# A 1,024-wide RWKV/S5 block with two trunk layers: the last gate projection before the last S5 output, a modulation group behind it

## The chip, the cores and the metric

One core of one Trainium2 chip runs the whole program. The metric is device time in microseconds (us) of one execution; the kernel before was run three times, and its median is 2729.56 us (2729.41 to 2731.32). The core has a matrix engine (TensorE, PE in the profile, with PEld for its weight loads), a vector engine (VectorE, DVE), an activation engine (ScalarE, ACT), a general engine (GpSimd, POOL) and a queue that issues transfers (SyncE, SP). Each engine runs its own instruction list in order, and the lists meet only at semaphores.

## The reference

The input is one sequence of 256 tokens of width 1,024, all in float32. A first block mixes it through two branches, each with a gate, and is followed by a convolutional FFN; then come two trunk layers (gated linear attention, latent attention, convolution, FFN) whose shifts and scales are made from a condition vector. The part that matters here, cut short:

```python
h = rms_norm(x, norm_mix_pre)
proj = h @ w_in                         # rwkv | s5 | gates
gates = sigmoid(proj[..., N_RWKV_COLS + S5_WIDTH:] + b_gate)
g_rwkv, g_s5 = split(gates, 2)          # 1,024 columns each
o_rwkv = rwkv7_branch(...) @ w_branch_rwkv
o_s5 = s5_branch(...) @ w_branch_s5
mixed = (g_rwkv * o_rwkv + g_s5 * o_s5) @ w_out
# s5_branch: a complex scan over time, y = Re(C @ states) + d * u,
#   y = gelu(y);  return y * sigmoid(y @ w_glu + b_glu)
# trunk layers: mod = silu(c) @ w_ada + b_ada   (6,144 columns, twice)
```

## The kernel before

Activations lie with channels on the 128 partitions and the 256 tokens along the free axis. All large weights are cut into tiles of 128x128; eight tiles are a slab of 512 KB, and the slabs lie in memory in the order in which TensorE uses them. SyncE loads slab after slab (L3732) into a ring of six; before it loads slab s it waits until slab s - 6 has been released by TensorE. A projection (`project`, matmul at L904) of 16 tiles takes two slabs and releases the first when it is through with it, the second at its end. A modulation group (`t_ada`, started by `more_ada`, matmul at L1794) multiplies the condition by 512 columns of `w_ada_2`; it takes 32 tiles, four slabs, and releases the four together at its end. All its groups add into one PSUM bank that stays held. No result of a group is read before the first FFN is under way, so a group can stand at many places of the list. The other seven PSUM banks are handed out in turn by `open_job`.

The order of work on TensorE is the order of calls in the list at the end of the program (from L3527 on). In the stretch of interest it is: a loop in which, for every two state tiles of the S5 branch, TensorE computes their inputs (`t_s5bu`, L1550) and one gate projection (`t_gate1`, L904), while VectorE runs the scans (`v_s5scan`, L1563 to L1582). There are eight gate projections of 256 columns, taken in the order GATE_ORDER = (4, 5, 6, 7, 0, 1, 2, 3), seven of them in this loop. After every fourth state tile `t_s5y` (L1593) multiplies the states by C. It waits for the last of the four scans. After the loop stand one modulation group, the last `t_s5y(3)`, and then `t_s5c`, the projection by `w_glu` (L904), which waits for the gelu of ScalarE (L1613), which waits for VectorE's addition of d * u (L1599). Then follow the low-rank products of the RWKV branch (`t_prep`, L1063 on, waiting for ScalarE's tanh at L1029), the Gram matrices (L1193), the triangular inversion (L1232), and the serial stage: four chunks of 64 tokens, each depending on the state of the one before (`t_serial`, L1321 to L1349). Behind it come the eighth gate projection, the group norm of y (`t_y`: L1394 needs ScalarE's copy of the last y at L1379; then two modulation groups; L1400 needs the squares at L1382), two more modulation groups, and `t_merge1`, the branch and output projections (L904), which needs `o_r`, VectorE's last product at L1418.

ScalarE has the same jobs in its own list. `a_gate1` (L1014) applies two sigmoids to a gate projection; the last of them stands in `a_y`, between the copies of y and the squares. Changing between sigmoid, gelu and the logarithm/exponential pair needs a table load on ScalarE. GpSimd loads `rows1`, the low-rank weights, once VectorE has done the addition for the last S5 output (L3709), and the trunk's context once `o_r` is done (L3711). The gates of the eighth projection are read for the first time in the last step of VectorE's merge (`v_merge1`, L1661).

Of the kernel before, what the change touches and what calls it, by code (L numbers as in the profile page):

```python
# [253 lines left out]
def build(nc, t_in, out, known):  # L254
# [3 lines left out]
    with ctx:  # L258
# [15 lines left out]
        def flat(a):  # L274
            return a.rearrange("p a b -> p (a b)")
# [30 lines left out]
        def pc(key, i=0, n=1):  # L306
            c = PCOL[(key, i)] if (key, i) in PCOL else PCOL[key + (i,)]
            return par[:, c:c + n]
# [12 lines left out]
        def at(step):  # L321

            return step_of(step)[1]
# [571 lines left out]
        def project(key, name, l, ms, kt, rhs, n, ready=None):  # L895


            o = open_job(key)
            for i, c in enumerate(ms):
                for k in range(kt):  # L900
                    if ready is not None and i == 0:
                        pe.wait_ge(*step_of(ready(k)))
                    w = tile(name, l, k * P, c)
                    ins = pe.matmul(o[:, i * n:(i + 1) * n], w, rhs(k), start=(k == 0), stop=(k == kt - 1))  # L904
                    slab_done(ins, i == len(ms) - 1 and k == kt - 1)
            ins.then_inc(tensor_jobs, close_job(key))
# [28 lines left out]
        def bank(key):  # L935
            return ps[:, job_of[key], :]
# [19 lines left out]
        def both_tables():  # L956

            act.add_instruction(mybir.InstLoadActFuncSet(name=nc.get_next_instruction_name(), engine=mybir.EngineType.Activation, act_func_set_id=LN_EXP_SET))
# [42 lines left out]
        def t_gate1(j):  # L1001
            c = NRW + RW + 2 * j * P
            project(("g", j), "w_in", 0, [c, c + P], DT, lambda k: h[:, k, :], TX)
# [7 lines left out]
        def a_gate1(j):  # L1011
            act.wait_ge(tensor_jobs, at(("job", ("g", j))))
            for e in range(2):
                act.activation(gates[:, 2 * j + e, :], bank(("g", j))[:, e * TX:(e + 1) * TX], ACT.Sigmoid,  # L1014
                                      bias=pc("b_gate", 2 * j + e)).then_inc(scalar_steps, A.step(("free", ("g", j)) if e else None))
# [149 lines left out]
        GATE_ORDER = (4, 5, 6, 7, 0, 1, 2, 3)  # L1165
# [210 lines left out]
        def a_y():  # L1376
            for c in range(4):
                act.wait_ge(tensor_jobs, at(("job", ("y", c))))
                act.copy(yR[:, :, c * 64:(c + 1) * 64], bank(("y", c))[:, 0:TX].rearrange("p (a b) -> p a b", b=64)).then_inc(scalar_steps, A.step(("free", ("y", c))))  # L1379
            a_gate1(GATE_ORDER[7])  # L1380
            act.wait_ge(vector_steps, at("yc"))
            act.activation(flat(ySq), flat(yC), ACT.Square).then_inc(scalar_steps, A.step("ysq"))  # L1382
            both_tables()
            for j in range(2):
                act.wait_ge(tensor_jobs, at(("job", ("yv", j))))
                act.activation(rstd[:, j, :], bank(("yv", j)), ACT.Ln, bias=eps_col[:, 1:2], scale=1.0 / 64).then_inc(scalar_steps, A.step(("free", ("yv", j))))
            act.wait_ge(scalar_steps, A.n)
            act.activation(flat(rstd), flat(rstd), ACT.Exp, scale=-0.5).then_inc(scalar_steps, A.step("yrstd"))
# [195 lines left out]
        def t_s5y(m):  # L1584

            if m == 0:
                pe.wait_ge(vector_steps, at("cneg"))
            pe.wait_ge(vector_steps, at(("xs", 4 * m + 3)))
            o = open_job(("ys", m))
            for g in range(4):  # L1590
                for q in range(4):
                    c_ = (s5c[:, 0], s5c[:, 1], s5c[:, 1], s5n)[g]
                    ins = pe.matmul(o[32 * q:32 * q + 32, 0:TX], c_[:, 4 * m + q, :], xs[:, q, g, :],  # L1593
                                    start=(g == 0), stop=(g == 3), skip_group_check=True)
            ins.then_inc(tensor_jobs, close_job(("ys", m)))
# [77 lines left out]
        def a_merge1():  # L1673
            for j in range(4):
                a_mixed("wo", "n2", j)
            a_rstd("n2")
# [123 lines left out]
        def more_ada(n=1):  # L1800
            for _ in range(n):
                t_ada(ada_done[0] // ADA, ada_done[0] % ADA)
                ada_done[0] += 1
# [1730 lines left out]
        @block.tensor  # L3534
        def _(tensor):
            nonlocal pe
            pe = tensor
            t_warm()
            t_norm("n1")
            t_proj1("u", (0, 1))  # L3540
            t_proj1("p", (0, 1))
            t_s5bt()
            t_proj1("p", (2, 3))
            t_s5bu(0)
            t_s5bu(1)
            t_proj1("p", (4, 5, 6))
            for p in range(8):
                if p % 2 == 0 and p:
                    t_s5y(p // 2 - 1)
                    more_ada()  # L3550
                if p < 7:
                    t_s5bu(2 * p + 2)
                    t_s5bu(2 * p + 3)
                if p < 7:
                    t_gate1(GATE_ORDER[p])
            more_ada()
            t_s5y(3)
            t_s5c()
            t_prep((more_ada, lambda: t_merge_s5((0, 1)), lambda: t_merge_s5((2, 3))))
            t_tr(("v",))  # L3560
            t_gram()
            t_tr(("At", "Bt", "Kt"))
            more_ada()
            t_chain()
            t_apply()
            t_serial()
            t_gate1(GATE_ORDER[7])
            t_y()
            more_ada(2)
            t_merge1()  # L3570
            more_ada()
            t_norm("n3")
            t_ffn1()
            for l in range(LAYERS):
                n = 512 if l == 0 else TX
                t_gla_in(l, n)
                t_gla(l)
                t_gla_out(l, n)
                t_branch_0(l)
                t_mla(l, n)  # L3580
                t_branch(l, n, 1, "mla_wo_2", lambda k: mO[:, k, 0:n], ahead=GATES_AHEAD)
                t_branch_c(l, n)
                t_wout(l, n)
                t_ln_close(("l1", l), n, more_ada if l == 0 else None)
                t_ffn2(l, n)
                t_ln_close(("l2", l), n)
            while len(stream) % SLAB:
                stream.append(None)

        @block.scalar  # L3590
        def _(scalar):
            nonlocal act
            act = scalar
            act.wait_ge(vector_steps, at("consts"))
            a_norm("n1", xT, ready=lambda k: "loaded_x%d" % (k // 4))
            act.wait_ge(loaded["par"], at("loaded_par"))
            a_s5a()
            a_proj1("u", (0, 1))
            a_proj1("p", (0, 1))
            a_s5bt()  # L3600
            a_cond()
            a_proj1("p", (2, 3, 4, 5, 6))
            for p in range(7):
                a_gate1(GATE_ORDER[p])
            a_s5c()
            a_prep()
            a_tr()
            for s in range(len(CHAIN)):
                if CHAIN[s][3] == "A":
                    for e in range(2):  # L3610
                        a_chain(s, e)
            a_apply()
            a_y()
            a_merge1()
            a_norm("n3", xT, ready=lambda k: ("n2", "res", k))
            a_ffn1()
            for l in range(LAYERS):
                n = 512 if l == 0 else TX
                if l == 0:
                    a_mod_half(1, range(4, DT))  # L3620
                    for k in range(DT):
                        act.wait_ge(vector_steps, at(("n4", "res", k)))
                        a_mod_half(0, (k,))
                a_gla_in(l, n)
                a_gla(l)
                a_gla_out(l, n)
                a_branch_0(l, n)
                a_mla(l, n)
                a_branch(l, n, 1, gtm, first=2)
                a_branch_c(l, n)  # L3630
                for m in (2, 4, 6):
                    for i in range(4):
                        a_pair_part(mix_pairs[l], ("wp", l, m), i)
                        if m == 6 and i in (1, 2):
                            a_ln_squares(("l1", l), n, range(3 * i - 3, 3 * i))
                a_ln_close(("l1", l), n, (l, 1), range(PIVOT + 2, DT))
                a_ffn2(l, n)
                a_ln_close(("l2", l), n, (l + 1, 0) if l + 1 < LAYERS else None)
# [196 lines left out]
```

## Time and profile before

| | us |
|---|---|
| median of the three runs (lowest, highest) | 2729.56 (2729.41, 2731.32) |
| the profiled execution | 2727.52 |
| its span, first to last instruction | 2725.3 |
| TensorE busy, matmuls | 2648.0 (97% of the span) |
| VectorE busy | 1818.7 (67%) |
| ScalarE busy | 783.6 (29%) |
| GpSimd busy | 86.4 (3%) |
| mean granted clock of TensorE | 0.992 of full speed |

All positions in time below are us from the start of the span. A matmul of 32-bit data is recorded as two instructions, so a projection of 16 tiles counts 32 of them.

### The profile page before, as it was taken

The numbers are of one execution on the slowest core, as the hardware profiler recorded it, in microseconds if no ns is written. First come the engines' busy times: TensorE is split into PE (matmuls) and PEld (weight loads), VectorE is DVE, ScalarE is ACT, GpSimd is POOL, SyncE is SP. The second block draws the span as 40 slices with busy tenths as digits, with TensorE's granted clock in tenths as the row PEclk, the third lists the DMA queues.
The fourth block names the chain that finished last, engine by engine and source line by source line (L and its number), as shares of the span: only waits on it lengthen the run. The fifth ranks groups of instructions, "written<-read, shape, count | busy, mean of one in ns | idle before, by whom it ended". The sixth has DMA issues, their size and how long they took to land. (4 is left out here: it accounts for less than half of the span.)

```text
span 2725.3 us, 42799 instructions
## 1 busy us (share of the span) xinstructions
PE 2648.0 (97%) x16876; PEld 2155.7 (79%) x16876; DVE 1818.7 (67%) x3740; ACT 783.6 (29%) x1684; POOL 86.4 (3%) x115
## 2 busy tenths in 40 slices
PE   9989999999999999999999999999998999999998
PEld 8768699988676868664457888888887977788998
DVE  7882289644787327886846776655539648768997
ACT  2132134132643122330121423301344322223431
POOL 0000000000221000000000000000003000000000
PEclk9999999999999999999999999999998999999999
DMA  5541644432331222212322222222320342243443
GB/s 206 183 166 69 249 165 170 171 128 87 131 134 70 93 70 93 70 62 70 108 70 93 106 80 93 85 101 93 113 78 25 132 132 70 87 143 142 171 166 129
DMA packets 86773, 313.62 MB, mean 115 GB/s; under 512 B 9472, under 2 KB 11520, under 8 KB 86320
## 3 DMA queue, kind: packets, MB, share of 16 engines
q1 hardware_dynamic: 85072, 304.25, 31.6%
q0 software_dynamic: 1504, 6.64, 0.7%
q8 instruction: 136, 2.23, 0.3%
q14 instruction: 61, 0.50, 0.1%
HBM read 309.81 MB, written 1.05 MB: 114 GB/s over the span
## 5 line engine op out<-in xcount | busy, mean ns | idle before, releaser
L601 PE MATMUL ps<-sb 128*128 128x128 f32 (+1 forms) x7560 | 1183.6, 319 | 5.1 <-ACT sb L677 3.3
L601 PEld LDWEIGHTS ps<-sb 128*128 128x128 f32 x7560 | 1096.1, 191 | 94.6 <-issue 5.8
L904 PE MATMUL ps<-sb 128*128 128x256 f32 (+1 forms) x2768 | 804.1, 448 | 7.0 <-DVE sb L983 3.7
L904 PEld LDWEIGHTS ps<-sb 128*128 128x128 f32 x2768 | 522.4, 190 | 271.3 <-issue 208.3
L2949 DVE SCALAR_TENSOR_TENSOR sb<-sb 128x512 f32<-128x512 f32 (+1 forms) x480 | 275.4, 615 | 8.7
L614 DVE TENSOR_TENSOR sb<-sb 128x512 f32<-128x512 f32 x146 | 100.3, 687 | 119.9 <-PE ps L601 88.0
L773 ACT COPY sb<-ps 128x256 f32<-128x256 f32 (+1 forms) x165 | 55.8, 338 | 324.7 <-PE ps L601 253.2
L677 ACT COPY sb<-ps 128x128 f32<-128x128 f32 (+1 forms) x252 | 75.3, 299 | 217.8 <-PE ps L601 214.4
L3519 DVE SCALAR_TENSOR_TENSOR sb<-sb 128x512 f32<-128x512 f32 (+1 forms) x176 | 101.0, 615 | 14.9 <-ACT sb L3465 9.9
L791 DVE TENSOR_TENSOR sb<-sb,ps 128x256 f32<-128x256 f32 (+1 forms) x90 | 34.0, 377 | 108.6 <-PE ps L601 73.9
L616 DVE TENSOR_TENSOR sb<-sb 128x512 f32<-128x512 f32 x146 | 101.0, 692 | 5.0
L710 PEld LDWEIGHTS ps<-sb 128*128 128x128 f32 x896 | 100.4, 192 | 0.1
L710 PE MATMUL ps<-sb 128*128 128x128 f32 x896 | 100.4, 275 | 0.0
L617 DVE TENSOR_TENSOR sb<-sb 128x512 f32<-128x512 f32 x146 | 99.8, 684 | 0.0
L619 DVE TENSOR_TENSOR sb<-sb 128x512 f32<-128x512 f32 x146 | 99.8, 684 | 0.0
L2247 POOL TENSOR_TENSOR sb<-sb 128x256 f32<-128x256 f32 x84 | 71.3, 885 | 376.8 <-ACT sb L2175 376.8
L1794 PE MATMUL ps<-sb 128*32 128x512 f32 x384 | 54.1, 599 | 10.2 <-DMA sb<-in_w 10.2
L3130 ACT ACTIVATE sb<-sb 128x256 f32<-128x256 f32 (+1 forms) x28 | 12.8, 507 | 166.4 <-DVE sb L3207 152.2
L2287 DVE COPY_PREDICATED sb<-sb,ps 64x128 f32<-64x128 uint32 x144 | 49.7, 345 | 11.8 <-PE ps L2079 2.4
L2213 DVE TENSOR_TENSOR sb<-sb 128x512 f32<-128x512 f32 x84 | 54.8, 723 | 3.3 <-ACT sb L2158 2.2
L2175 ACT ACTIVATE sb<-sb 128x256 f32<-128x256 f32 x168 | 54.3, 414 | 4.8 <-DVE sb L2213 4.8
L3465 ACT ACTIVATE sb<-sb 128x512 f32<-128x512 f32 (+1 forms) x84 | 54.9, 703 | 0.2
(457 smaller groups left out, 2651.9 us busy)
## 6 DMA issues: line engine op xcount, KB each, us to landing
sb<-in_w SPq DMA_DIRECT2D x574, 512.0 KB, 3.6
sb<-in_two POOLq DMA_DIRECT2D x2, 1088.0 KB, 7.9
sb<-in_x SPq DMA_DIRECT2D x2, 512.0 KB, 4.7
sb<-in_ctx POOLq DMA_DIRECT2D x1, 1024.0 KB, 9.0
sb<-in_v_bias POOLq DMA_DIRECT2D x2, 512.0 KB, 4.0
sb<-in_par SPq DMA_DIRECT2D x1, 764.0 KB, 6.6
sb<-in_s5b POOLq DMA_DIRECT2D x1, 512.0 KB, 8.0
sb<-in_s5c POOLq DMA_DIRECT2D x1, 512.0 KB, 10.0
```

The lines of the kernel that those rows point to most:

```text
L601: ins = pe.matmul(o, w, xs(i), start=(fresh and i == 0), stop=(i == len(ws) - 1), skip_group_check=True)
L614: ve.tensor_tensor(buf[:, 0], half(s2, 0), half(s2, 1), ALU.add).then_inc(vector_steps, V.step(("S1", key)))
L616: ve.tensor_tensor(buf[:, 1], buf[:, 0], half(s1, 0), ALU.subtract).then_inc(vector_steps, V.step(("S2", key)))
L617: ve.tensor_tensor(half(s2, 0), half(s1, 0), half(s2, 0), ALU.subtract).then_inc(vector_steps, V.step(("S3", key)))
L619: ve.tensor_tensor(buf[:, 2], half(s1, 1), buf[:, 1], ALU.subtract).then_inc(vector_steps, V.step(("S4", key)))
L677: act.copy(f.part[:, i, :], bank((key, bk))[:, 0:f.hn]).then_inc(scalar_steps, A.step((name, key)))
L710: ins = pe.matmul(o[:, tt * P:(tt + 1) * P], xs(i)[:, tt * P:(tt + 1) * P], w, start=(fresh and i == 0 and tt == 0), stop=(i == len(ws) - ...
L773: act.copy(dst, src).then_inc(scalar_steps, A.step((name, key)))
L904: ins = pe.matmul(o[:, i * n:(i + 1) * n], w, rhs(k), start=(k == 0), stop=(k == kt - 1))
L2247: po.tensor_tensor(halves(QK[:, :, lev, :], lev, d), halves(kT[:, :, tok], lev, d), halves(E[:, :, lev, :], lev, d), ALU.mult).then_inc(po ...
L2949: ve.scalar_tensor_tensor(out=o_, in0=s_, scalar=pc(("conv_dw", l, j), m + e), in1=o_, op0=ALU.mult, op1=ALU.add).then_inc(vector_steps, V ...
L3519: ve.scalar_tensor_tensor(out=o_, in0=z2[e][:, g, 0:c, j:j + TX], scalar=pc(("ffn_dw", l, j), g * FT + m), in1=o_, op0=ALU.mult, op1=ALU.a ...
```

## The change

The eighth gate projection (index 3 of the gates, by GATE_ORDER[7]) leaves its place behind the serial stage and goes behind the loop, ahead of the last S5 output. The modulation group that stood ahead of that output goes behind it. On ScalarE the eighth pair of sigmoids moves along, to the end of the loop of gates and ahead of the gelu. The order of the weights in memory is made from the order of use, so the slabs move along too. Nothing else is changed: the instructions are the same in number and kind.

```diff
@@ a_y (ScalarE)
                 act.copy(yR[:, :, c * 64:(c + 1) * 64], bank(("y", c))[:, 0:TX]...)
-            a_gate1(GATE_ORDER[7])
             act.wait_ge(vector_steps, at("yc"))
@@ the list of TensorE
                 if p < 7:
                     t_gate1(GATE_ORDER[p])
+            t_gate1(GATE_ORDER[7])
+            t_s5y(3)
             more_ada()
-            t_s5y(3)
             t_s5c()
             t_prep((more_ada, lambda: t_merge_s5((0, 1)), lambda: t_merge_s5((2, 3))))
...
             t_serial()
-            t_gate1(GATE_ORDER[7])
             t_y()
             more_ada(2)
             t_merge1()
@@ the list of ScalarE
-            for p in range(7):
+            for p in range(8):
                 a_gate1(GATE_ORDER[p])
             a_s5c()
```

## Rows read from the trace of the kernel before

**Rows 1.** The page, part 1: engine, busy us, share, instructions.
```profile
PE 2648.0 (97%) x16876; PEld 2155.7 (79%) x16876; DVE 1818.7 (67%) x3740; ACT 783.6 (29%) x1684; POOL 86.4 (3%) x115
```

**Rows 2.** Waits of TensorE: line, waited for, us, times, longest.
```profile
PE ps L1794 <- DMA sb<-in_w: 10.2, 13, 2.4
```

**Rows 3.** TensorE's timeline around the previous S5 output: start, us, line, count.
```profile
114.02 1.94 PE L1593 MATMUL ps<-sb 128*32 128x256 f32 x32
115.78 1.90 PE L1794 MATMUL ps<-sb 128*32 128x512 f32 x16
117.61 1.14 PE L1550 MATMUL ps<-sb 32*128 32x256 f32 x8
```

**Rows 4.** TensorE's timeline around the last S5 output.
```profile
138.62 7.17 PE L904 MATMUL ps<-sb 128*128 128x256 f32 x32
145.72 1.92 PE L1794 MATMUL ps<-sb 128*32 128x512 f32 x16
151.28 3.30 PE L1593 MATMUL ps<-sb 128*32 128x256 f32 x32 [3.64 <-DVE sb L1582]
156.28 7.20 PE L904 MATMUL ps<-sb 128*128 128x256 f32 x32 [1.70 <-ACT sb L1613]
164.71 1.34 PE L1063 MATMUL ps<-sb 64*128 64x256 f32 x5 [1.23 <-ACT sb L1029]
```

**Rows 5.** Timeline of VectorE and ScalarE, 140 to 168.
```profile
145.83 0.84 ACT L1014 ACTIVATE sb<-ps,sb 128x256 f32<-128x256 f32 x2 [10.92 <-PE ps L904]
...
146.69 1.28 ACT L1613 ACT_TABLE_LOAD   x1
...
154.66 0.48 DVE L1599 SCALAR_TENSOR_TENSOR sb<-sb,ps 128x256 f32<-128x256 f32 x1 [3.04 <-PE ps L1593]
155.17 1.06 ACT L1613 ACTIVATE sb<-sb 128x1024 f32<-128x1024 f32 x1 [7.20 <-DVE sb L1599]
```

**Rows 6.** Stretches: window, length, busy by engine, PEclk, DMA share, GB/s.
```profile
151.20:154.70 3.50, 3.30 (x32) 1.39 (x32) 0.46 (x3) 0.00 (x0) 0.00 (x0) 0.59 0.92 366
...
240.00:257.00 17.00, 16.14 (x224) 14.73 (x222) 7.80 (x19) 1.13 (x3) 0.00 (x0) 1.00 0.01 2
...
273.00:286.00 13.00, 9.75 (x40) 1.70 (x36) 5.06 (x7) 2.43 (x3) 0.91 (x1) 1.00 0.95 360
```

**Rows 7.** ScalarE's timeline, 0 to 60: a table load and what follows it.
```profile
41.71 1.28 ACT L1534 ACT_TABLE_LOAD   x1
43.00 0.56 ACT L1534 ACTIVATE sb<-sb 128x432 f32<-128x432 f32 x1
```

**Rows 8.** DMA issues by tensor, whole span: KB each, median us to landing.
```profile
sb<-in_s5c POOLq DMA_DIRECT2D x1, 512.0 KB, 10.0
sb<-in_rows POOLq DMA_DIRECT2D x1, 512.0 KB, 3.8
```

**Rows 9.** TensorE's timeline behind the serial stage.
```profile
257.01 7.17 PE L904 MATMUL ps<-sb 128*128 128x256 f32 x32
264.02 1.88 PE L1394 MATMUL ps<-sb 128*128 128x512 f32 x4
265.84 2.90 PE L1794 MATMUL ps<-sb 128*32 128x512 f32 x24
271.18 1.05 PE L1794 MATMUL ps<-sb 128*32 128x512 f32 x4 [2.44 <-DMA sb<-in_w]
...
286.17 27.97 PE L904 MATMUL ps<-sb 128*128 128x256 f32 x128 [0.34 <-DMA sb<-in_w]
```

**Rows 10.** Timeline of ScalarE and VectorE, 248 to 290.
```profile
257.13 0.37 ACT L1379 COPY sb<-ps 128x256 f32<-128x256 f32 x1 [3.69 <-PE ps L1349]
...
281.23 1.22 DVE L1418 TENSOR_TENSOR sb<-sb 128x1024 f32<-128x1024 f32 x1
```

**Rows 11.** Slab loads (L3732) issued between 267.8 and 268.3.
```profile
L3732 SPq DMA_DIRECT2D sb<-in_w x2: 328/380/433, 267.8 to 268.2; - x2
...
DMA to landing us min/median/max: 3.3/3.8/4.2
```

## Prediction

> **What bounds the kernel now.** The page comes first: TensorE's matmuls are busy for 2648.0 us of a span of 2725.3 [rows 1]. The change removes no instruction, so it can bring only what it takes out of TensorE's 77 us without a matmul, or out of stretches in which a matmul takes longer than it must. TensorE's waits come next: 10.2 us of them are for weights ahead of modulation groups [rows 2]. Then TensorE's own timeline at both places of the change. At the front place it ends a modulation group, stands 3.64 us until VectorE's last scan is done, runs the last S5 output in 3.30 us, stands 1.70 us for the gelu, and goes on with the `w_glu` projection at 156.28 [rows 4]. At the back place it runs the eighth gate projection from 257.01, then the mean of y from 264.02 without a gap, then modulation groups that wait for weights, and from 286.17 the branch projections [rows 9]. So the front place has idle time beside a cheap group, and the back place has a projection on which nothing near it waits. The span runs on TensorE at both, and the question is how much of 7.1 us (the step from one projection's start to the next job's, 138.62 to 145.72 [rows 4]) disappears in front, and how much is won behind.
>
> The previous S5 output took 1.94 us where the last one takes 3.30 [rows 3, 4]. The windows give the reason: in 151.2 to 154.7, right behind the wait, the granted clock is 0.59, so for most of it the lower level of 1.2 GHz instead of 2.4 [rows 6]. The wait thus costs 3.64 us and another 1.36 us.
>
> **The change, part by part: the front.** I set up the new order from 145.72, where the loop's last projection gives over, with steps between starts from the same jobs elsewhere.
>
> - Gate projection: 32 recorded matmuls, step 7.10 [rows 4]. The next job can start at 152.82. It needs weights of two slabs; in the old order TensorE took four slabs at this very place with no wait, so two are there.
> - Last S5 output: VectorE's scan was done by 151.28 [rows 4], so there is no wait, and no idle time ahead of it that would bring the clock down. It takes 1.94 us, step 1.76 [rows 3]: its last matmul ends at 154.76, and the modulation group starts at 154.58.
> - Modulation group: 16 matmuls, step 1.83 [rows 3]. TensorE is free at 156.41. Its four slabs go into places of the ring that were released by 145.8 at the latest, nine microseconds ahead.
> - Gelu: VectorE followed the old output's end (151.28 + 3.30 = 154.58) by 0.08, ScalarE's gelu followed VectorE's start by 0.51, took 1.06, and TensorE followed it by 0.05 [rows 4, 5]. From 154.76 that gives 154.84, 155.35, 156.41, and the `w_glu` projection at 156.46.
>
> Old 156.28, new 156.46: the front pays 0.18 us for a projection of 7.1. What hides it is the 3.64 us wait, the 1.70 us wait (now behind the modulation group) and the 1.36 us of the lower clock, together 6.7 us; steps account for the rest.
>
> On ScalarE the eighth sigmoids stand ahead of the gelu. Two take 0.84 us, starting 0.04 after the projection's last matmul, and the table load of 1.28 follows after 0.02 [rows 4, 5]. From the end at 152.89: sigmoids 152.93 to 153.77, load 153.79 to 155.07. The gelu's input is there at 155.35, so the load has 0.28 us to spare. In a load with work waiting behind it, the next activation started 1.29 us after the load's start [rows 7]. The Trainium skill, "ScalarE: Activation LUTs", section "What ACT_TABLE_LOAD costs", speaks against this: about 1283 ns of load and a further 1380 ns of drain, "~2.66 µs total" for a switch. By that the gelu would start at 156.45 and the projection at 157.56, and the front would cost 1.28 us instead of 0.18. The load's length agrees with the trace; the drain is not to be seen there.
>
> Every queue that moves: SyncE's loads follow the new order. The front place now releases two slabs in the projection (one half way, one at 152.9) and four at about 156.5, where the old order released four at about 147.7. The next user of those four is a modulation group at about 169.7, and a load lands in some 3.3 to 4.2 us [rows 11], so this is hidden by nine microseconds. GpSimd's load of `rows1` starts when VectorE's addition for the last S5 output ends, 0.18 later than before, and now has the four slabs for neighbours. It landed in 3.8 us; it is needed for L1063 at 164.71, some nine microseconds after its issue. The nearest row of a load of this size that had to share is `in_s5c` with 10.0 us [rows 4, 8]. Bounds: nothing (3.8 again) to 0.7 us late (10.0 from 155.6, against 164.9). I take nothing, because twice the time of its own row would still be in time. VectorE's and ScalarE's chains of `v_prep` and `a_prep` start 0.18 later and shift as a whole. PSUM banks are handed out in turn and the number of jobs over the whole stretch is the same, so behind it every job has its old bank; inside it each bank's former user is seven jobs back and long read.
>
> **The change, part by part: behind the serial stage.** The projection goes, step 264.02 - 257.01 = 7.01 us [rows 9]. What is late next: ScalarE's copy of the last y, 257.13 to 257.50 [rows 10], on which the mean waits and which the projection covered. With the 0.05 us from ScalarE to TensorE seen above, the mean starts at 257.55 instead of 264.02: 6.47 us earlier. The table load for the sigmoid that followed that copy goes too, and lay on no path. From the other side: if the mean's first weight load, which can't be pulled ahead under the projection any more, costs a further 0.3 us, it is 6.2. I take 6.47.
>
> Then the modulation groups. They wait for weights, so I have to ask whether the loads come earlier too. In the 17 us ahead of 257 the DMA share is 0.01 [rows 6]: the ring is full at 257, with all six slabs loaded. In the old order two of those belong to the projection, and the two that replace them load under it. In the new order the full ring holds the first six slabs of the modulation groups straight away. In both, 24 matmuls (six slabs) run at once, and the wait of 2.44 us comes at the seventh [rows 9]. That one was issued at 267.8 [rows 11], which is the end of the first group of four slabs (265.84 + 1.83 = 267.67), since a group releases its slabs only together. So each later landing hangs on the start of the modulation groups and not on the projection, and all of it up to 286.17 moves by the same 6.47. `o_r` is done at 281.23 + 1.22 = 282.45 [rows 10], before the weights, and moves along. The stretch behind is the same work in the same order.
>
> **The sum**: + 0.18 - 6.47 = - 6.29 us. On the profiled execution's own 2727.52 that is 2721.23. The median of the three runs lies 2.04 us above that execution; by the median it is 2729.56 - 6.3 = **2723.3 us**. With the bounds above (0 to + 0.7 for `rows1`, 0 to + 0.3 for the mean), and one of the short stretches of lower clock more or less, worth up to 1.4 us as at the last S5 output, the main case spans 2721.5 to 2725.5.
>
> **The rivals.**
>
> *The weights decide behind the serial stage.* If a transfer bounds that stretch, the projection was filling time in which slabs came, and removing it brings them no sooner. For it: DMA share 0.95 and 360 GB/s in 273 to 286 [rows 6]. The price: the two slabs loaded under the projection would now have to be fetched in the starved part, where the rate of 360 GB/s makes 1.46 us of each 0.524 MB; 2.9 us of the 6.3 are lost, by the median 2726.2. Against it: the ring is full at the start in both orders, so the slabs to be fetched before 286 are fewer by two. Chance 0.08.
>
> *More is won.* Without the idle time in front, and with a busier TensorE behind it, another stretch of lower clock in the Gram matrices is not granted. That is worth what the last S5 output shows, 1.4 us: 2721.9. Nothing in the order there changes, only a shift by 0.18. Chance 0.07.
>
> *The switch of tables or `rows1` is late in front.* + 1.1 or + 0.7 us, 2724.0 to 2724.4. Against it are the rows already named. Chance 0.07.
>
> *The clock, on the other side: slower.* Behind the serial stage the projection is 7 us of dense work just ahead of groups with gaps. Without it, TensorE goes from the serial stage over a short wait into the first gap of 2.44 us, and the clock could fall there and stay low into the 28 us of branch projections. At the lower level the last S5 output took 1.36 us more in a stretch of 3.30, and projections without waits would take twice their time, so each microsecond of work so prolonged costs one: the gain of 6.3 is gone from 6.3 us of projections at full speed (12.6 at half) on. If it lasted for 14 us of them, the time is 2729.56 - 6.3 + 14 = 2737.3. Against it: the same gaps, with TensorE busy 9.75 of 13 us, had a granted clock of 1.00 [rows 6]; the lower stretch in front followed an unbroken idle of 3.64 us. Chance 0.03.
>
> *The change doesn't do what it says.* If the eighth projection were needed sooner than I read, or VectorE's scans slowed with TensorE working beside them, the front would pay more. The scans ran beside projections throughout the loop, so little speaks for it; 2 to 3 us lost, 2726. Chance 0.05.
>
> **How the numbers follow.** The main case has the remaining 0.70, at 2723.3. The range takes in the first three rivals and leaves out the clock: 2720.8 to 2726.5. What a measurement can tell from no change here is 0.2%, 5.5 us, so "faster" is below 2724.1. The main case's centre is only 0.8 us inside of that, and the runs before spread over 1.9 us; I give it 0.9 of its chance: 0.63. With the case of more gain, and a fraction of the table case, faster is 0.72. Same takes the rest of these, the weights and the failure in front: 0.25. Slower is the clock case: 0.03.
>
> **What would show it.** In the new trace L1593 for the last S5 output takes about 1.9 us, with no wait or a negligible one, and the clock there is 1.00. The `w_glu` projection starts within 0.3 us of 156.46, still released by the gelu or just behind the modulation group. The mean (L1394) starts 6.3 us earlier than 264.02, with a wait of half a microsecond for L1379. The wait of 2.44 us at the seventh slab is still there, and the branch projections start at about 279.9. I am wrong if that wait grows by about the amount removed (weights), if the granted clock behind 257 falls below 1.00 (clock), or if the projection by `w_glu` starts later than 157.5 (front).

## The result, and the profile after

| | before | after |
|---|---|---|
| median of 20 runs, us | 2732.69 | 2720.52 |
| lowest, highest, us | 2724.39, 2748.57 | 2717.36, 2734.78 |
| ratio of the runs compared, 95% interval | | 0.9952 (0.9936 to 0.9968) |

The change makes the kernel faster by 0.5%, about 12 us between the medians and 9 to 17 us by the interval. The forecast was 2723.3 us, a gain of 6.3, with a range from 2720.8. The time fell 0.3 us under the range, and the gain is nearly twice the forecast; the base of three runs (2729.56) was also low for this kernel, whose median came out at 2730 to 2733 in every later comparison.

The first profiled execution of the changed kernel took 2734.62 us, far from its median: runs of both kernels fall into two groups some 15 us apart, and in that one the granted clock was 0.56 from 236 to 262, through the serial stage. I therefore read the changed kernel from a second profile (2720.94 us, span 2718.9) taken with the first experiments. TensorE at the front place, as start, duration, line, count, and idle time ahead with who ended it:

```profile
138.59 14.08 PE L904 MATMUL ps<-sb 128*128 128x256 f32 x64
152.60 1.94 PE L1592 MATMUL ps<-sb 128*32 128x256 f32 x32
154.36 1.90 PE L1793 MATMUL ps<-sb 128*32 128x512 f32 x16
156.23 7.20 PE L904 MATMUL ps<-sb 128*128 128x256 f32 x32
164.66 1.34 PE L1063 MATMUL ps<-sb 64*128 64x256 f32 x5 [1.23 <-ACT sb L1029]
```

Two gate projections stand in a row, the last S5 output (now L1592) takes 1.94 us with no wait, and the `w_glu` projection starts 17.64 us after the first of the two, where it started 17.66 us after the only one before [rows 4]. The eighth projection is hidden to the last tenth of a microsecond. ScalarE had the gelu's tables in time, in the second profile's rows of ScalarE and VectorE:

```profile
153.56 1.28 ACT L1612 ACT_TABLE_LOAD   x1
154.61 0.48 DVE L1598 SCALAR_TENSOR_TENSOR sb<-sb,ps 128x256 f32<-128x256 f32 x1 [3.02 <-PE ps L1592]
155.12 1.06 ACT L1612 ACTIVATE sb<-sb 128x1024 f32<-128x1024 f32 x1 [0.28 <-DVE sb L1598]
```

The load ends at 154.84 and the gelu starts at 155.12, released by VectorE. The drain of a further 1.38 us that the Trainium skill ("ScalarE: Activation LUTs", "What ACT_TABLE_LOAD costs") adds would have put it at 156.2; it is not there, as in [rows 7]. Behind the serial stage, TensorE in the same profile:

```profile
253.88 3.54 PE L1393 MATMUL ps<-sb 128*128 128x512 f32 x4 [0.47 <-ACT sb L1379]
257.34 2.78 PE L1793 MATMUL ps<-sb 128*32 128x512 f32 x24
262.70 1.05 PE L1793 MATMUL ps<-sb 128*32 128x512 f32 x4 [2.58 <-DMA sb<-in_w]
...
279.50 10.81 PE L904 MATMUL ps<-sb 128*128 128x256 f32 x49 [2.05 <-DMA sb<-in_w]
```

The mean follows ScalarE's copy after 0.47 us of idle time, and the wait for the seventh slab is there as in [rows 9]. But the mean takes 3.54 us instead of 1.88, at the lower clock (0.54 from 253.9 to 257.3). Set side by side, the distances between first starts of the stages, in us, from the timelines of two profiles of each kernel:

| from, to | before (2727.5) | before, 2nd (2729.6) | after, 2nd (2720.9) | after, 1st (2734.6) |
|---|---|---|---|---|
| last projection of the loop but the moved one, low-rank products | 26.09 | 28.23 | 26.07 | 26.07 |
| these, Gram matrices | 24.99 | 24.99 | 25.00 | 24.99 |
| Gram matrices, inversion | 15.81 | 13.75 | 11.78 | 11.79 |
| inversion, serial stage | 35.14 | 35.96 | 35.53 | 36.11 |
| serial stage, mean of y | 23.37 | 23.37 | 16.91 | 28.53 |
| mean, variance | 9.43 | 10.21 | 11.96 | 11.90 |
| variance, branch projections | 12.72 | 13.18 | 13.66 | 13.58 |

The row of the serial stage holds the forecast: 23.37 - 16.91 = 6.46 us, where 6.47 was foreseen. The last two rows take part of it back: from the mean to the branch projections it is 25.62 us where it was 22.15 and 23.39. From there to the end of the span both kernels take the same time: 2439.2 to 2439.4 us in the first three columns (2440.9 in the fourth). The row of the Gram matrices was not in the forecast at all. There, with no instruction moved in or out, 2 to 4 us are gained. In the first column the granted clock was 0.78 from 189 to 200, in the second profile of after it was 1.00:

```profile
189.00:200.00 11.00, 7.88 (x329) 7.27 (x326) 9.01 (x16) 1.08 (x2) 0.00 (x0) 0.78 0.16 52
```

```profile
189.00:200.00 11.00, 9.68 (x355) 8.11 (x357) 10.03 (x17) 4.18 (x8) 0.00 (x0) 1.00 0.16 51
```

But the clock doesn't explain where TensorE stands still. The Gram matrices (L1193), first before, then after:

```profile
189.70 2.20 PE L1193 MATMUL ps<-sb 64*64 64x64 f32 x135
194.26 3.06 PE L1193 MATMUL ps<-sb 64*64 64x64 f32 x127 [2.35 <-issue]
198.09 1.96 PE L1193 MATMUL ps<-sb 64*64 64x64 f32 x58 [0.76 <-issue]
```

```profile
189.66 3.60 PE L1193 MATMUL ps<-sb 64*64 64x64 f32 x230
194.53 1.61 PE L1193 MATMUL ps<-sb 64*64 64x64 f32 x90 [1.27 <-issue]
```

"Issue" says that the profile names no engine and no transfer that ended the wait. TensorE's lines before had the sum of these waits as well, 3.1 us ahead of L1193:

```profile
L1193 PE MATMUL ps<-sb 64*64 64x64 f32 x320 | 7.2, 259 | 3.1 <-issue 3.1
```

The 320 matmuls are the same, and the wait stands elsewhere: 135 and 127 more before, 230 after. That is 32 less than 135 + 127 = 262, and the moved projection has 32 recorded matmuls (and 32 weight loads). Numbering all of TensorE's recorded instructions in the traces, 34,949 in either kernel, I find the waits behind numbers 2,240 and 2,496 before, and behind 2,496 after; the first instruction of the Gram matrices is number 1,969 before and 2,034 after. The page has a queue for instructions:

```profile
q8 instruction: 136, 2.23, 0.3%
```

136 packets, in the trace of 16,384 bytes each: 2.23 MB over 34,949 instructions is 64 bytes each, and a packet is 256 instructions. TensorE's list comes in blocks of 256, and 2,496 - 2,240 = 256.

The packets lie in the trace with their times, so the waits can be laid beside them (us):

| | before, 1st | after, 2nd |
|---|---|---|
| the Gram matrices start | 189.70 | 189.66 |
| a packet of the instruction queue | 191.98 to 192.94 | 183.14 to 184.10 |
| TensorE stands behind number 2,240 | 191.91 to 194.26 | not at all |
| the next packet | 195.39 to 196.64 | 191.94 to 193.19 |
| TensorE stands behind number 2,496 | 197.32 to 198.09 | 193.26 to 194.53 |

In the kernel before, the packet behind number 2,240 starts 2.3 us after the Gram matrices do, when TensorE has just run out. In the changed kernel it has landed 5.6 us before they start. The three waits end 1.32, 1.45 and 1.34 us after a packet's end.

Two theories for what the forecast had missed were put to the test. **Fetch**: the Gram matrices take 16 ns for a recorded matmul with its weight load (230 in 3.60 us), so they use a block of 256 up in 2 us; from their start to the end of the first wait it is 4.56 us. They run dry if the fetch comes only once they have begun. The 65 instructions moved ahead of them bring one fetch ahead of their start. **History**: the idle time in front brings the clock down there, and the clock is likelier to be low further on.

### The profile page after: what moved, and what is told of

Read it like the earlier page. It is cut to its first block and busy times, and to the rows that moved or that the text cites. A ratio compares the mean times of both kernels' runs of the same rounds, so it can differ in the third digit from the quotient of the medians.

```text
span 2732.6 us, 42798 instructions
## 1 busy us (share of the span) xinstructions
PE 2662.4 (97%) x16876; PEld 2167.0 (79%) x16876; DVE 1818.5 (67%) x3740; ACT 781.6 (29%) x1683; POOL 86.5 (3%) x115
## 3 DMA queue, kind: packets, MB, share of 16 engines
q8 instruction: 136, 2.23, 0.3%
## 5 line engine op out<-in xcount | busy, mean ns | idle before, releaser
L3129 ACT ACTIVATE sb<-sb 128x256 f32<-128x256 f32 (+1 forms) x28 | 12.8, 507 | 166.4 <-DVE sb L3206 152.1
```

## The experiments

They ran in three sets, each on one chip, with the kernel before beside them (medians 2731.53, 2731.01 and 2731.78 us). Times are medians; where two kernels other than before are compared I give the 95% interval of the difference of medians, resampled from the runs. Some of these pairs come from different sets, which the intervals don't cover.

**The changed kernel again**, as the base.

> The changed kernel once more, as the base for the three experiments beside it. By the first comparison (20 runs each) it should be about 10 us faster than before in the runs without a long stretch of lower clock (medians 2719.9 and 2729.8), and 10 to 13 us over all. Schedule theory: 6.5 us of it are fixed (6.47 behind the serial stage, 0 in front) and the rest comes from the clock. If the fixed part is all that is real, this time the lower cluster should stand 6 to 7 us below the one of before.

2720.63 us (12 runs) against 2731.53 (35), ratio 0.9960 (0.9947 to 0.9974). The gain of 10.9 us is clear of noise (7 to 14.5 us by the interval), and more than the 6.5 us that the schedule theory fixes.

**Without the eighth projection**: before, the projection left out (its gates are zero; its PSUM bank is skipped, which the cut below leaves out, like ScalarE's part).

```diff
             t_serial()
-            t_gate1(GATE_ORDER[7])
             t_y()
```

> The kernel before with the eighth gate projection left out altogether (its 256 gate columns are zero); the order in front is that of before, with its idle time. Schedule theory: the projection is hidden entirely in the changed kernel, so this one has the same time as the changed one, 6.5 us below before. History theory (the idle time in front brings the clock down there and makes it likelier to fall again in the Gram matrices, the inversion and the serial stage): this one gains the 6.5 us only, and the changed kernel is faster than it by 3 to 4 us in the lower cluster, and has its long slow stretch more rarely.

2726.54 us, ratio 0.9987 (0.9968 to 1.0006): 5.0 us below before. The changed kernel, which does the projection, is 5.9 us faster than this one, which doesn't (3.7 to 15.3). So by the medians about half of the gain doesn't come from hiding the projection. Its trace has the Gram matrices of before (135, 127, 58), with the clock high, and 13.65 us to the inversion:

```profile
189.74 2.21 PE L1199 MATMUL ps<-sb 64*64 64x64 f32 x135
194.20 2.09 PE L1199 MATMUL ps<-sb 64*64 64x64 f32 x127 [2.25 <-issue]
197.69 1.14 PE L1199 MATMUL ps<-sb 64*64 64x64 f32 x58 [1.40 <-issue]
```

**At both places**: the changed kernel, with the projection a second time at the old place (a helper of the same content; its definition and ScalarE's part are left out).

```diff
             t_serial()
+            t_gate_again(GATE_ORDER[7])
             t_y()
```

> The changed kernel with the eighth gate projection done a second time at its old place behind the serial stage, into the same gates. In front it is the changed kernel, behind it is the one before. Schedule theory: the time of before, within 1 us. History theory: 3 to 4 us below before, since only the front tells the two apart.

2729.87 us, 0.9994 (0.9976 to 1.0012); 1.7 us below before and 9.2 (7.2 to 11.5) above the changed kernel. Its Gram matrices are those of after (230, 90; 11.78 us). The 9.2 are more than the projection's 6.5, and neither theory gives them. Between the two profiled executions the difference is 6.3 us (2727.22 against 2720.94); what makes it larger in the medians stays open.

**Idle time filled**: before, eight matmuls ahead of the last S5 output's wait.

```diff
+            o = open_job(("ys", m))
+            if m == 3:
+                for k in range(DT):
+                    pe.matmul(o[:, 0:TX], C["ident"], h[:, k, :], ...)
             pe.wait_ge(vector_steps, at(("xs", 4 * m + 3)))
-            o = open_job(("ys", m))
```

> The kernel before with eight matmuls of identity by the normed input put into the idle time ahead of the last S5 output (about 3.5 us of dense work, their result is overwritten), everything else as before. Schedule theory: the last S5 output takes 1.94 us instead of 3.30 and the w_glu projection starts 1.4 us earlier: 1.4 us below before. History theory: 1.4 us and another 2 to 3 us by the clock further on, as in the experiment with the projection at both places.

2730.95 us, 1.0003 (0.9979 to 1.0027). In the trace the low-rank products start 24.72 us after the loop's last projection instead of 26.09, the 1.37 foreseen; in the median nothing of it can be told. The filling adds 31 recorded instructions, and the Gram matrices break where the fetch theory has it, 15 matmuls sooner:

```profile
188.41 1.98 PE L1193 MATMUL ps<-sb 64*64 64x64 f32 x120
192.52 2.11 PE L1193 MATMUL ps<-sb 64*64 64x64 f32 x127 [2.14 <-issue]
195.97 1.32 PE L1193 MATMUL ps<-sb 64*64 64x64 f32 x73 [1.33 <-issue]
```

The clock was high here from the front to the inversion, and the two waits are there all the same (before had 2.35 and 0.76 us in one profile, 2.08 and 1.68 in the other). They are not of the clock's making.

**Before again**, for a second profile.

> The kernel before once more, for a second profile of it: its first profiled execution (2727.52 us) lay below the median of its runs (2731.5), so the changed kernel's gain of 10.9 us in the medians can't be read off the two traces alone. Expected: the median of before within 1 us. Fetch theory (TensorE's instructions come in blocks, and in the Gram matrices it outruns them where a block begins just behind the wait that opens them): the Gram matrices again fall into 135, 127 and 58 recorded matmuls with idle time between, and the inversion starts 13.5 us (clock high) to 16 us (clock low) after the Gram matrices' start. The other 3 to 4 us of the median: in a stretch of lower clock between 240 and 290, which the first profile of before did not have.

2730.07 us, 0.9995 (0.9979 to 1.0011). The Gram matrices were as expected. The lower clock lay for the most part elsewhere than expected. Between 262 and 290 it was 0.94, which made mean to variance 10.21 us instead of 9.43. The larger part lay in front: from 151.2 to 154.7 it was 0.50, from 156.3 to 161 still 0.58, and the `w_glu` projection behind the idle time took 9.01 us instead of 7.20:

```profile
151.21 3.64 PE L1593 MATMUL ps<-sb 128*32 128x256 f32 x32 [3.63 <-DVE sb L1582]
156.54 9.01 PE L904 MATMUL ps<-sb 128*128 128x256 f32 x32 [1.69 <-ACT sb L1613]
```

```profile
156.30:161.00 4.70, 4.46 (x12) 3.66 (x13) 4.55 (x11) 1.47 (x2) 0.00 (x0) 0.58 0.37 114
```

So the idle time of 3.64 us costs 1.4 us by the clock in one execution and 3.5 in another, all of which is gone in both profiles of the changed kernel (26.07 us in the first row of the table).

**Only 64 instructions more** (63 in the record): the kernel without the eighth projection, with 16 matmuls of 16 columns in the idle time.

```diff
+            o = open_job(("ys", m))
+            if m == 3:
+                for _ in range(16):
+                    pe.matmul(o[:, 0:16], C["ident"], C["ones"][:, 0:16], ...)
             pe.wait_ge(vector_steps, at(("xs", 4 * m + 3)))
-            o = open_job(("ys", m))
```

> The kernel before without the eighth projection (its gates zero), as in the experiment that left it out, and with 16 matmuls of 16 columns in the idle time ahead of the last S5 output; they do nothing but bring TensorE's instruction list ahead of the Gram matrices to the length that it has in the changed kernel (64 instructions more). Fetch theory: the Gram matrices fall into 230 and 90 recorded matmuls, the inversion starts 11.8 us after their start instead of 13.7, and the time is 2 to 4 us below the kernel that only leaves the projection out (2726.5), at 2722 to 2724. History theory (the idle time in front is what costs): it is still there, so no difference from 2726.5.

2723.53 us, 0.9979 (0.9960 to 0.9998). In the trace the pattern of after appears, and 11.77 us to the inversion instead of 13.65:

```profile
190.01 3.60 PE L1199 MATMUL ps<-sb 64*64 64x64 f32 x231
194.89 1.55 PE L1199 MATMUL ps<-sb 64*64 64x64 f32 x89 [1.28 <-issue]
```

Work of no use ahead of a wait makes the stage of the Gram matrices 1.9 us shorter; that shows the fetch. The front did not stay as it was, though. The small matmuls took up the idle time whole, and the last S5 output behind them was as slow as behind the idle time:

```profile
147.65 3.89 PE L1596 MATMUL ps<-sb 128*128 128x16 f32 x32
151.47 3.41 PE L1601 MATMUL ps<-sb 128*32 128x256 f32 x32
```

The granted clock was 0.56 from 151.5 to 154.9. In the filling with the normed input, 3.72 us of matmuls of 256 columns at this place left it at 1.00.

The median is 3.0 us below the kernel without the 64 instructions, but with 12 runs each this difference has no sure sign (-12.8 to +8.2). The changed kernel lies another 2.9 us lower (0.1 to 14.1). The lower clock in front, which this kernel keeps, may be the cause, but it is not shown: the profiled executions of the two are equal within 0.5 us (2720.45 and 2720.94).

**Alignment spoilt**: the changed kernel with 192 instructions more near its start.

```diff
             t_warm()
+            for _ in range(24):
+                pe.matmul(ps[:, BANKS - 1, 0:16], C["ones"], C["ones"][:, 0:16], ...)
             t_norm("n1")
+            for _ in range(24):
+                pe.matmul(ps[:, BANKS - 1, 0:16], C["ones"], C["ones"][:, 0:16], ...)
```

> The changed kernel with 48 matmuls of 16 columns in the idle times around the first norm, at about 6 and 11 us (192 instructions), so that the first instruction of the Gram matrices stands as far ahead of the end of a block as in the kernel before. Fetch theory: the pattern of 135, 127 and 58 comes back although the front is that of the changed kernel, the inversion starts 13.5 to 16 us after the Gram matrices' start, and the time is 2 to 4 us above the changed kernel (2720.6). History theory: no difference but up to 1 us for the 48 matmuls.

2736.43 us, 1.0018 (0.9996 to 1.0040). The total says little: a recorded matmul of 16 columns took 0.11 us, as long as its weight load, and the padding by itself delayed the low-rank products by 10.7 us. But the pattern of before is back in the changed kernel, with 13.92 us to the inversion:

```profile
200.30 2.20 PE L1193 MATMUL ps<-sb 64*64 64x64 f32 x134
204.73 2.93 PE L1193 MATMUL ps<-sb 64*64 64x64 f32 x127 [2.22 <-issue]
208.06 1.61 PE L1193 MATMUL ps<-sb 64*64 64x64 f32 x59 [0.40 <-issue]
```

**Without the exchange of the group**: the projection moved, the modulation group left ahead of the S5 output.

```diff
+            more_ada()
             t_s5y(3)
-            more_ada()
             t_s5c()
```

> The changed kernel with the modulation group left ahead of the last S5 output, so only the eighth projection is moved. Schedule theory: the S5 output starts 1.83 us later, the gelu's 1.70 us lie open again, and the w_glu projection starts 1.9 us later; 1.9 us above the changed kernel (2720.6), at 2722.5. The Gram matrices keep the pattern of 230 and 90, since the number of instructions ahead of them is the same. History theory: no long idle time in front, so nothing beyond the 1.9 us.

2722.87 us, 0.9963 (0.9945 to 0.9982), 2.2 us above the changed kernel (0.5 to 5.3). The gelu's wait is open again and the front takes 1.72 us more (27.79 instead of 26.07):

```profile
158.00 7.20 PE L904 MATMUL ps<-sb 128*128 128x256 f32 x32 [1.69 <-ACT sb L1612]
```

This trace also shows the stretch behind the serial stage at full clock throughout (1.00 from 253 to 290):

```profile
255.71 1.99 PE L1393 MATMUL ps<-sb 128*128 128x512 f32 x4 [0.47 <-ACT sb L1379]
265.16 1.99 PE L1399 MATMUL ps<-sb 128*128 128x512 f32 x4
279.10 11.24 PE L904 MATMUL ps<-sb 128*128 128x256 f32 x51 [0.95 <-DMA sb<-in_w]
```

Mean to variance is 9.45 us, as in the first profile of before (9.43), but variance to branch projections is 13.94 instead of 12.72, and a weight slab ends the wait. The kernel with 64 instructions more has 14.13 there, at full clock as well.

**Better versions.** The first moves one of the two groups between mean and variance ahead of the serial stage.

```diff
             t_apply()
+            more_ada()
             t_serial()
@@ t_y
-            more_ada(2)
+            more_ada()
             pe.wait_ge(scalar_steps, at("ysq"))
```

> The changed kernel with one of the two modulation groups between the mean of y and its variance moved ahead of the serial stage, where DMA is idle. It costs 1.83 us there, of which 0.7 lie in a wait. Behind, one group of 1.83 us fits between the mean and the variance without waiting for weights, so the variance starts 2 us after the group's start instead of 7.6, o_r is ready 9 us after that, and the four slabs fewer let the branch projections start at about 14 us behind the mean instead of 22 to 25. In sum 5 to 7 us below the changed kernel (2720.6): 2714 to 2716. If the weights decide there throughout, only 1.1 us are lost and the rest is as before: 2721 to 2722.

2716.43 us (6 runs), 0.9937 (0.9914 to 0.9961), 4.2 us below the changed kernel (1.5 to 6.9), a little less than foreseen. Mean to variance now takes 3.86 us instead of 11.96, and the branch projections start 7.3 us earlier. In this profile 5.0 of these are lost again behind them, 1.7 of them in one projection (8.83 us instead of 7.14) that follows a wait of 2.05 us. The second puts the group that stood ahead of the inversion into the Gram matrices, on top of that.

```diff
@@ t_gram
             for n, lh, rh in GRAM:
+                if n == "rb":
+                    more_ada()
@@ the list of TensorE
             t_tr(("At", "Bt", "Kt"))
-            more_ada()
             t_chain()
```

> The kernel with one group moved ahead of the serial stage (2716.4), with in addition the group that stood between the Gram matrices and the inversion put inside the Gram matrices, ahead of their fourth product. Fetch theory: the group's 1.83 us of slow work lie in the time in which the next block of instructions comes, the wait of 1.3 to 1.5 us in the Gram matrices goes, and the inversion starts 10.3 to 10.5 us after their start instead of 11.8: 1.3 us lower in all, at 2715. Without a limit by instructions: the same time.

2711.29 us (6 runs), 0.9921 (0.9897 to 0.9945). The group is inside, and the wait in the Gram matrices is gone; the inversion starts 10.03 us after their start instead of 11.77:

```profile
189.83 3.03 PE L1195 MATMUL ps<-sb 64*64 64x64 f32 x192
192.79 1.93 PE L1795 MATMUL ps<-sb 128*32 128x512 f32 x16
194.64 2.10 PE L1195 MATMUL ps<-sb 64*64 64x64 f32 x128
```

The gain over the first, 5.1 us (2.0 to 7.7), is more than the 1.3 us expected. The waits for instructions further on changed too: in the inversion the first had 1.98 and 0.54 us, this one 1.14 and 0.25, and the mean starts 3.3 us earlier. The rest of the gain stays open. The third takes the group from behind the variance instead.

```diff
@@ the list of TensorE, on top of the second
             t_tr(("At", "Bt", "Kt"))
+            more_ada()
             t_chain()
...
             t_y()
-            more_ada(2)
+            more_ada()
             t_merge1()
```

> As the last one, but the group inside the Gram matrices is taken from the two behind the variance of y, and the one between Gram matrices and inversion stays. In the Gram matrices it costs 0.4 us net. Behind, the branch projections now wait for o_r and not for weights: they start 9.1 us after the variance (ScalarE and VectorE's chain of before: 273.45 to 282.45) instead of 12.3 us. In sum 2.5 to 3 us below the kernel with one group moved: 2713.5. If weights come late for the group between Gram matrices and inversion (its last two slabs are released 5 us ahead), up to 1 us of that is lost.

2712.72 us (6 runs), 0.9924 (0.9898 to 0.9951). The branch projections do wait for `o_r` and no longer for weights, 9.05 us after the variance:

```profile
273.33 16.85 PE L904 MATMUL ps<-sb 128*128 128x256 f32 x69 [3.35 <-DVE sb L1419]
```

The 3.2 us won there (12.28 in the first) don't show in the whole: there is one group more ahead of the mean, and in this profile, the slowest of the six runs, the clock fell at the mean. In the medians it can't be told from the second (-1.4 to +4.4). The second, 9.3 us below the changed kernel (7.4 to 10.8), is the best of all.

## Why the prediction was right and where it failed

**The front** was right. The projection costs nothing there (-0.02 us; + 0.18 foreseen), the S5 output takes 1.94 us without a wait, and the exchange of the group is worth 1.7 us in the trace. The switch of tables is in time.

**Behind the serial stage** the removal was right: 6.46 us for 6.47. The wait at the seventh slab did not grow by the amount removed, so the rival of the weights did not come true as it was priced. But the clause that "all of it up to 286.17 moves by the same 6.47" failed: mean to branch projections took 25.6 us where it was 22.2 and 23.4 before. Of the 3.5 us against the first profile, 1.7 are the mean at the lower clock, so the sign named for the rival of the clock was there, in small. Clock and weights share the rest: even with the clock at 1.00 the branch projections started 1.2 us later behind the mean (23.4 us) than in the first profile of before, waiting for a slab. The second profile of before had 23.4 as well, with a stretch of lower clock, so the traces don't show whether the removal makes the weights later. The clock fell at the mean in three of the nine profiles without a projection ahead of it (in a fourth it was low already), and in none of the four with one; that points to the removal, but doesn't prove it. (Of the two loads that the prediction put under the projection, the second was issued behind it, at 264.22; nothing waited for it.)

The large form of this rival, a clock at 0.56 through the serial stage, occurs in some runs, and of before as well. In the first comparison 9 of 20 runs of before lay above 2737 us and 4 of 20 of after above 2730; beside the first experiments it was 8 of 35 and 1 of 12. Whether the change makes it rarer, these runs don't settle.

**What failed is the step that let the stretch between the two places "shift as a whole"**, and so put the Gram matrices at nothing in the sum; with it failed the rival that gave "more is won" 0.07 and only 1.4 us because nothing in the order there changes but a shift by 0.18. The shift in time is indeed nothing. What changed is the shift in number: 65 instructions more ahead of the Gram matrices. It takes away the first of two waits for instructions, 1.9 us with the clock high in both kernels (13.65 against 11.77, without the eighth projection in both), and 4.0 us against the first profile of before, where the clock fell behind the wait. The rows of TensorE's lines before showed the wait, as "issue" ahead of L1193, and the prediction left it out. The history theory found no support: with the idle time in front filled, both waits stayed and the median did not move.

**One size was off as well**: the clock behind the idle time in front, priced at 1.36 us from the S5 output alone. In the second profile the lower clock went on into the `w_glu` projection, which makes 3.5 us. The prediction took one execution for the rule. The same holds for its base: three runs gave 2729.56 us, the 20 that these three belong to gave 2732.69. (Its bounds for the main case, 2721.5 to 2725.5, come out of its own terms as 2721.9 to 2725.7.)

The traces can be summed up to the branch projections. Against the first profile of before the changed kernel gains 6.5 us in the serial stage and 4.0 in the Gram matrices, nothing in front, and loses 0.4 in the inversion and 3.5 behind the mean: 6.6 us, and the executions differ by 6.6 (2727.52 and 2720.94). Against the second it gains 6.5, 2.0, 2.2 in front and 0.4 in the inversion, and loses 2.2 behind the mean: 8.8 us before rounding, and the executions differ by 8.6. So the forecast for the profiled execution, 2721.23, came within 0.3 us of 2720.94, but by luck: a gain that it did not have and a loss that it did not have nearly cancel.

The medians differ by more, 10.9 and 12.2 us, and by 9.9 (2729.8 and 2719.9) between the runs of the first comparison below 2737 and 2730 us. By the medians the 10.9 us divide into 5.0 for the projection's absence behind, 3.0 for the 64 instructions and 2.9 for the rest, each by one comparison with a wide interval. That the Gram matrices lost a wait for instructions, and how long it was, is shown; what makes the medians 2 to 6 us further apart than the profiled executions is not.

## What to carry to other kernels

Where a stage issues many small matmuls, count TensorE's instructions and look for idle time put down to "issue" at numbers 256 apart: moving work from behind that stage to ahead of it moves these waits, and slower work put inside hides them. An idle stretch on TensorE cost its length and then some by the clock here, a different amount in each execution; price it from several profiles, and take a base from more than three runs. Work that needs nothing nearby is well placed where the engine already waits. Taking it away from its old place removes its own time, but what follows it can wait for something else or run at the lower clock: follow the new trace up to the point from which both kernels take the same time.

## What the runs showed of the hardware

- TensorE's instructions arrive in packets of 16,384 bytes, 256 instructions of 64 bytes. The waits for them stood behind recorded numbers 2,240, 2,496, 2,752, 3,008, 3,264, 3,520, 4,800 and 5,056 in one kernel or another, all of them 2,240 and a multiple of 256, wherever the code had been moved. In the Gram matrices they lasted 0.4 to 2.4 us. In all thirteen traces they ended 1.2 to 1.6 us after a packet of that queue had ended.
- A product of 128x128 weights by 16 columns of 32-bit data took 0.11 us per recorded matmul, as much as its weight load: 48 of them 5.43 us.
- Behind 3.64 us of idle time TensorE's granted clock was 0.59 in one profile and 0.50 in another; behind 3.89 us in which it did nothing but products of 16 columns it was 0.56; behind 3.72 us of products of 256 columns it was 1.00.
- A table load on ScalarE that ended 0.28 us ahead of its activation delayed it by nothing.
